# Sparse attention's value products: the two key/value heads in the array's two column halves in turn

## The chip, the cores and the metric

The kernel runs on one core of a Trainium2 chip. A core has a matrix engine (TensorE, PE), a vector engine (VectorE, DVE), a scalar engine (ScalarE, ACT), GpSimd (POOL), and SyncE (SP), which here only issues DMA transfers. Each engine works through its own instruction stream in order and they wait for each other through semaphores. PE loads a stationary operand (a weight load, PEld in the profile) and streams the moving operand past it (a matmul, PE), and writes only to PSUM, which has 8 banks of 128 partitions. The metric is the device time of the whole program in microseconds (us), the median of three runs.

## The reference

Two transformer blocks over 256 positions of width 1024, batch 1. The change lies in the second block's mixer, which adds a sparse attention (NSA) with 8 query heads in 4 groups over 2 key/value heads of width 64, and a gated linear attention (GLA) with 4 heads, each behind a branch projection and a gate:

```python
o_nsa = nsa_attention(q_a, kc, vc, ks_, vs_, kw, vw, gate_a + nsa_gate_b[l], ...)
o_gla = gla(q_b, k_b, v_b, r_b, alpha_b, gla_w_alpha2[l], gla_b_alpha[l], gla_norm_g[l])
g_nsa, g_gla = jnp.split(jax.nn.sigmoid(merge), 2, axis=-1)
mix = g_nsa * (o_nsa @ w_branch_nsa[l]) + g_gla * (o_gla @ w_branch_gla[l])
x = x + (mix @ w_out[l]).astype(x.dtype)
```

Inside `nsa_attention` each query head has three outputs, over compressed keys, selected blocks and a window, added with gates:

```python
o_cmp = jnp.einsum('bhgqn,bnhd->bqhgd', p_cmp.astype(v_cmp.dtype), v_cmp)
...
o_slc = jnp.einsum('bhgqk,bhqkd->bqhgd', p_slc.astype(vg.dtype), vg)
...
o_win = jnp.einsum('bhgqk,bkhd->bqhgd', p_win.astype(vwb.dtype), vwb)
return gb[..., 0:1] * o_cmp + gb[..., 1:2] * o_slc + gb[..., 2:3] * o_win
```

With 256 positions there are 4 blocks of 64 keys, all of them selected, and the window covers 256 positions, so both are dense causal attentions here. GLA works in chunks of 64 positions: `o_intra` (a masked 64x64 product with v) plus `o_inter` (the queries with the state of all chunks before).

## The kernel before

Every large product is split into exact high and low parts (three matmuls, `mm3`); the small attention products run in fp32, each of which the profile records as two passes, a weight load and a matmul each. All work is planned by a `Schedule` that writes steps into one list; each engine's program runs through this list and picks its own steps, so the order on each engine is fixed when the program is built. A step takes PSUM banks through `use`, and PE's `open_bank` waits until the bank's last reader has released it.

Weights come in units of 1 MB through a ring of four slots (`low_f`): SP loads unit u when PE has finished unit u - 4, ACT writes its rounded part (`high`), DVE the rest (`low_r`), each in two halves of 128x1024, and then PE uses it. `planned` loads four row blocks of 128 rows as `(k p) n -> p k n`, so row block k holds rows 128k to 128k + 127.

The stretch of interest is written by `nsa`, woven with `gla` and with a stream of wide projection steps (`fill`: the merge gates, then the GLA branch weights "bg"). A head index n (0 to 7) stands for one query half i = n // 4 (128 queries) and one group g = n % 4, both key/value heads v at once. For each n the steps are:

- `nsa_s` (PE): scores, both value heads in two row halves of the array. DVE adds the slopes and takes maxima, ACT exponentials, DVE (`nsa_w`) the gated weights.
- `nsa_t` (PE): turns these weights into banks 6, 7 and 1 (128x128 blocks, and one 64x128 for the compressed ones). ACT copies them to `WK_f`: the transposed weights, per v at column 2048 + 512v, the compressed ones at 3072.
- `nsa_v` (PE): the value products. For each v: for both branches and each key tile (nk = i + 1 tiles) one product of the values `VSW` (128 rows, 64 columns) with the turned weights, and one of the compressed values `VC2`, which uses 47 rows. Both v write the same 64 partitions `hr` of bank 1 (lower half for even g, upper for odd), v = 0 into columns 0 to 127 and v = 1 into 128 to 255.
- ACT copies 64x256 elements of it to `ONT`, high part, and DVE subtracts for the low part. `head_pair` says where: partitions `hr`, row blocks g // 2 and g // 2 + 2, so that `ONT`'s four row blocks stand in the reference's row order.

After the last head the branch projection "bn" takes `ONT` as stationary operand against the units of `w_branch_nsa_2`.

In GLA, for a pair i of chunks, `gla_t` computes the intra-chunk scores for two row halves p (banks 0 and 1), two products each. `gla_o` computes, for p = 0 and then p = 1: two products with 128 rows (`AT` with `VB`), then for each chunk n = 2i + half two products of 64 rows and 64 columns, queries with `STATE`, into partitions 64half. Chunk 0 has no state, so pair 0 has one such half and pair 1 both.

The names in the rows: `PS` is PSUM; `AR_f` and `AR_r` are one large work area that holds VSW, VC2, ONT, EN, QB, STATE, AT and more; `HT_r` the turned activations; `XN` the GLA output. Shapes such as 128*64 are rows and columns of the stationary operand.

Of the kernel before, what the change touches and what calls it, by code (L numbers as in the profile page):

```python
# [11 lines left out]
ALU = mybir.AluOpType  # L12
# [121 lines left out]
class Schedule:  # L134
# [23 lines left out]

    def plan_wide(self, key, w, c0, n=1024):
        for c in range(c0, c0 + n, 512):  # L160
            for k0 in range(0, w.shape[0] // 128, 4):
                self.planned(key, w, k0, 4, c, 512)
# [14 lines left out]
    def make_plan(self, A):  # L177
# [26 lines left out]
        for key, w in (("bg", A["w_branch_gla_2"][0]), ("bn", A["w_branch_nsa_2"][0])):  # L204
            for c in range(0, 1024, 512):
                self.planned(key, w, 0, 4, c, 512)
# [809 lines left out]
def two_blocks(nc, A, out):  # L1016
    ctx = ExitStack()
    with ctx:
# [105 lines left out]
        VSW = ar(1536, 2, 2, 128)  # L1124
# [135 lines left out]
        def head_pair(n):  # L1260

            i, g = divmod(n, 4)
            hr = slice(64 * (g % 2), 64 * (g % 2) + 64)
            return ONT[hr, g // 2:4:2, i * 128:i * 128 + 128]
# [41 lines left out]
        def tensor_program(eng):  # L1306
# [408 lines left out]
            def gla_t(s):  # L1715
                i = s["i"]
                pe.wait_ge(s_gel, 1)
                for p in range(2):
                    use = U["gt", i, p]
                    rr = slice(64 * p, 64 * p + 64)  # L1720
                    open_bank(use)
                    for q in range(2):
                        m = mm(bank(use)[:, 128 * q:128 * q + 128], EN[rr, q, 128 * i:128 * i + 128],
                               QB[rr, q, 128 * i:128 * i + 128], True, True)
                    m.then_inc(use.full[0], 1)

            def gla_o(s):
# [4 lines left out]
                for p in range(2):  # L1732
                    use = U["go", i, p]
                    open_bank(use)
                    for q in range(2):
                        h = 2 * q + p
                        m = mm(bank(use)[:, 128 * q:128 * q + 128], AT[:, 2 * p + q, :],
                               VB[:, i, 128 * h:128 * h + 128], q == 0, False)
                    for half in range(2):
                        n = 2 * i + half  # L1740
                        if n == 0:
                            continue
                        pe.wait_ge(*U["gs", n - 1].read)
                        for q in range(2):
# [3 lines left out]
                    m.then_inc(use.full[0], 1)  # L1748
# [49 lines left out]
            def nsa_v(s):  # L1798
# [4 lines left out]
                hr = slice(64 * (g % 2), 64 * (g % 2) + 64)  # L1803
# [6 lines left out]
                open_bank(use)  # L1810
                for v in range(2):
                    oo = bank(use)[hr, 128 * v:128 * v + 128]
                    wT = wk(2048 + 512 * v, 512)
                    for br in range(2):
                        for kt in range(nk):
                            j = br * nk + kt
                            mm(oo, VSW[:, br, kt, 64 * v:64 * v + 64], wT[:, 128 * j:128 * j + 128], j == 0, False)
                    m = mm(oo, VC2[0:47, v, :], wk(3072, 128)[0:47, :], False, True)
# [1607 lines left out]
```

## Time and profile before

| | |
|---|---|
| median of 3 runs | 830.67 us (829.7 to 832.2) |
| span of the profiled execution | 829.0 us |
| PE busy | 816.5 us, 98% of the span |
| weight loads busy | 704.3 us, 85% |
| DVE / ACT / POOL busy | 610.5 / 455.6 / 96.6 us |
| DMA | 143.40 MB, mean 173 GB/s |
| granted TensorE clock | 1.000 |
| the stretch with the sparse attention's heads | about 453 to 558 us |

The times come from one profiled execution. PE's matmuls are pipelined: the recorded duration of one is longer than the distance to the next, so costs are read from the distance between starts. The weight loads of short products start in step with their matmuls, so the start of a group of loads tells when its products begin.

### The profile page before, as it was taken

How to read it: one execution, taken by the hardware profiler on the slowest of the kernel's cores; microseconds unless marked ns; L12 is line 12 of the kernel's file. 1: busy time of each engine (PE TensorE's matmuls, PEld its weight loads, DVE VectorE, ACT ScalarE, POOL GpSimd, SP SyncE). 2: the span in 40 equal slices, each digit the busy share in tenths (PEclk: the TensorE clock that was granted, in tenths of full speed). 3: DMA queues.
4: the chain of work that ended last, by engine and by line, in shares of the span. 5: the costliest groups of instructions: out<-in, count | busy, mean ns of one | idle time of the engine just before them, and what ended most of it. 6: DMA issues, size and time to landing. Idle time of an engine off the chain costs nothing.

```text
span 829.0 us, 12090 instructions
## 1 busy us (share of the span) xinstructions
PE 816.5 (98%) x4841; PEld 704.3 (85%) x4841; DVE 610.5 (74%) x966; ACT 455.6 (55%) x804; POOL 96.6 (12%) x106
## 2 busy tenths in 40 slices
PE   7999999999999999999999999999999999999997
PEld 6878888888888888899998777778888999999886
DVE  6878767978877755567578776858568799998744
ACT  6656565735555544454575546554476645544533
POOL 4200000000000000000400000000000455655100
PEclk9999999999999999999999999999999999999999
DMA  9854634555755555374875333244543556555551
GB/s 331 231 174 135 225 119 153 175 189 167 253 173 184 203 189 173 146 249 129 241 218 171 120 102 102 102 151 163 171 150 102 184 172 203 165 192 183 177 199 51
DMA packets 81607, 143.40 MB, mean 173 GB/s; under 512 B 5090, under 2 KB 35840, under 8 KB 81552
## 3 DMA queue, kind: packets, MB, share of 16 engines
q1 hardware_dynamic: 79232, 137.11, 50.7%
q0 software_dynamic: 2160, 5.46, 2.3%
q8 instruction: 38, 0.62, 0.3%
q14 instruction: 17, 0.14, 0.0%
q10 hardware_dynamic: 160, 0.07, 0.0%
HBM read 141.05 MB, written 1.05 MB: 171 GB/s over the span
## 4 chain that ended last, share of the span: by engine, by line
PE 96%; DVE 2%; ACT 1%; DMA 0%; issue 0%; ACTq 0%; DVEq 0%
PE PS L1310 92%; PE PS L1324 4%; ACT WK_f L1928 1%; DMA VR<-in_norm_attn_g_dram 0%; DVE low_r L2439 0%; DVE HT_r L2439 0%; ACT high L1931 0%; DVE WK_f L2443 0%; DVE X L2439 0%; ACT AR_f L1931 0%; DVE WK_f L2447 0%; DVE AR_f L2439 0%; DVE XN L2443 0%; DVE AR_f L2443 0%; DVE WK_f L2439 0%
## 5 line engine op out<-in xcount | busy, mean ns | idle before, releaser
L2439 DVE TENSOR_TENSOR low_r<-low_f,high 128x1024 fp32r<-128x1024 f32 (+1 forms) x256 | 325.7, 1314 | 77.4 <-ACT high L1931 77.2
L1931 ACT ACTIVATE high<-low_f 128x1024 fp32r<-128x1024 f32 (+1 forms) x264 | 257.4, 1024 | 76.0 <-DMA low_f<-in_w_down_dram 35.0
L1310 PE MATMUL PS<-HT_r,high 128*128 128x256 f32 (+2 forms) x1232 | 267.5, 308 | 0.0
L1310 PE MATMUL PS<-high,AR_r 128*128 128x512 f32 (+2 forms) x724 | 214.9, 377 | 0.0
L1310 PEld LDWEIGHTS PS<-HT_r,high 128*128 128x128 f32 (+1 forms) x1232 | 199.7, 190 | 12.2
L1310 PE MATMUL PS<-HT_r,low_r 128*128 128x256 f32 (+1 forms) x712 | 200.9, 282 | 0.0
L1310 PE MATMUL PS<-high,HT_r 128*128 128x512 f32 (+1 forms) x576 | 189.3, 396 | 0.7 <-DVE HT_r L2439 0.4
L1310 PEld LDWEIGHTS PS<-high,AR_r 128*128 128x128 f32 (+1 forms) x724 | 129.2, 181 | 26.4 <-issue 0.5
L1310 PEld LDWEIGHTS PS<-HT_r,low_r 128*128 128x128 f32 (+1 forms) x712 | 135.2, 190 | 0.0
L1310 PE MATMUL PS<-low_r,AR_r 128*128 128x512 f32 (+2 forms) x362 | 134.0, 374 | 0.0
L1310 PEld LDWEIGHTS PS<-high,HT_r 128*128 128x128 f32 x576 | 108.0, 189 | 25.1 <-issue 2.7
L1310 PE MATMUL PS<-low_r,HT_r 128*128 128x512 f32 (+1 forms) x288 | 110.9, 387 | 0.0
L1310 PEld LDWEIGHTS PS<-low_r,AR_r 128*128 128x128 f32 (+1 forms) x362 | 65.5, 181 | 12.1
L3246 POOL TENSOR_TENSOR WK_f<-WK_f 128x512 f32<-128x512 f32 x33 | 53.3, 1616 | 115.2 <-DVE WK_f L2447 113.4
L1310 PEld LDWEIGHTS PS<-low_r,HT_r 128*128 128x128 f32 x288 | 54.7, 190 | 9.3
L1931 ACT ACTIVATE AR_r<-AR_f 128x512 fp32r<-128x512 f32 (+1 forms) x29 | 18.2, 629 | 71.6 <-DVE AR_f L2439 40.6
L2439 DVE TENSOR_TENSOR AR_r<-AR_f,AR_r 128x512 fp32r<-128x512 f32 (+1 forms) x29 | 23.7, 822 | 18.9 <-ACT AR_r L1931 18.9
L1928 ACT ACTIVATE WK_f<-WK_f,st 128x128 f32<-128x128 f32 (+2 forms) x80 | 32.9, 416 | 6.0 <-DVE st L2443 6.0
L1310 PE MATMUL PS<-AR_f 64*128 64x128 f32 (+5 forms) x268 | 31.9, 318 | 0.2 <-ACT AR_f L1931 0.2
L1310 PEld LDWEIGHTS PS<-AR_f 64*128 64x128 f32 (+2 forms) x268 | 24.6, 182 | 8.5 <-issue 6.7
L1931 ACT ACTIVATE AR_f<-PS 128x512 f32<-128x512 f32 (+2 forms) x34 | 18.7, 550 | 21.7 <-PE PS L1310 20.2
L1931 ACT ACTIVATE WK_f<-PS 128x512 f32<-128x512 f32 (+2 forms) x38 | 15.3, 448 | 26.7 <-PE PS L1324 23.9
(173 smaller groups left out, 694.9 us busy)
## 6 DMA issues: line engine op xcount, KB each, us to landing
low_f<-in_w_in_dram SPq DMA_DIRECT2D x39, 1024.0 KB, 5.2
low_f<-in_w_up_dram SPq DMA_DIRECT2D x38, 1024.0 KB, 5.2
low_f<-in_w_down_dram SPq DMA_DIRECT2D x27, 1024.0 KB, 4.9
low_f<-in_w_out_dram SPq DMA_DIRECT2D x8, 1024.0 KB, 5.0
low_f<-in_w_xkv_dram SPq DMA_DIRECT2D x4, 1024.0 KB, 5.7
low_f<-in_w_branch_gla_dram SPq DMA_DIRECT2D x2, 1024.0 KB, 5.0
low_f<-in_w_branch_nsa_dram SPq DMA_DIRECT2D x2, 1024.0 KB, 5.0
low_f<-in_w_xq_dram SPq DMA_DIRECT2D x2, 1024.0 KB, 5.4
```

Source lines behind the costliest of these rows:

```text
L1310: return nc.tensor.matmul(o, l, r, start=start, stop=stop, skip_group_check=True)
L1324: return nc.tensor.transpose(o, i, ident[0:n, 0:n])
L1928: return nc.scalar.activation(o, i, f, bias=bias, scale=scale, accum_out=total)
L1931: return nc.scalar.activation(o, i, ACT.Copy, bias=0.0, scale=1.0)
L2439: return nc.vector.tensor_tensor(o, a, b, op)
L3246: return nc.gpsimd.tensor_tensor(o, a, b, op)
```

## The change

The value products of head n put value head v into column half v of the array: `oo[v]` are the partitions 64v to 64v + 63 of the bank, and both write columns 0 to 127. The products of the two value heads stand in turn. The compressed product uses all 128 rows of `VC2` and of the turned weights, whose other rows are cleared once. The output, now 128x128, is copied and subtracted as one block, and `ONT` has one row block for each g, with the two value heads as its halves. `by_value_head` loads the branch weights in that row order, each unit as two loads of 64 partitions. In `gla_t` and `gla_o` the products of the row halves stand in turn, and `gla_o`'s 128-row products come ahead of all its 64-row ones.

```diff
@@ class Schedule
+    def by_value_head(self, key, w, c):
+
+        def half(v):
+            src = w[256 * v:256 * v + 256, c:c + 512].rearrange("(g d) n -> d g n", d=64)
+            return lambda a: v3(a, 4, 512)[64 * v:64 * v + 64], src
+
+        self.unit(key, 4, 512, [half(v) for v in range(2)])
@@ make_plan
-        for key, w in (("bg", A["w_branch_gla_2"][0]), ("bn", A["w_branch_nsa_2"][0])):
-            for c in range(0, 1024, 512):
-                self.planned(key, w, 0, 4, c, 512)
+        for c in range(0, 1024, 512):
+            self.planned("bg", A["w_branch_gla_2"][0], 0, 4, c, 512)
+        for c in range(0, 1024, 512):
+            self.by_value_head("bn", A["w_branch_nsa_2"][0], c)
@@ head_pair
-            hr = slice(64 * (g % 2), 64 * (g % 2) + 64)
-            return ONT[hr, g // 2:4:2, i * 128:i * 128 + 128]
+            return ONT[:, g, i * 128:i * 128 + 128]
@@ gla_t, PE
                 for p in range(2):
-                    use = U["gt", i, p]
-                    rr = slice(64 * p, 64 * p + 64)
-                    open_bank(use)
-                    for q in range(2):
+                    open_bank(U["gt", i, p])
+                for q in range(2):
+                    for p in range(2):
+                        use = U["gt", i, p]
+                        rr = slice(64 * p, 64 * p + 64)
                         m = mm(bank(use)[:, 128 * q:128 * q + 128], EN[rr, q, 128 * i:128 * i + 128],
                                QB[rr, q, 128 * i:128 * i + 128], True, True)
-                    m.then_inc(use.full[0], 1)
+                        if q == 1:
+                            m.then_inc(use.full[0], 1)
@@ gla_o, PE
-                        m = mm(bank(use)[:, 128 * q:128 * q + 128], AT[:, 2 * p + q, :],
-                               VB[:, i, 128 * h:128 * h + 128], q == 0, False)
-                    for half in range(2):
-                        n = 2 * i + half
-                        if n == 0:
-                            continue
-                        pe.wait_ge(*U["gs", n - 1].read)
-                        for q in range(2):
+                        mm(bank(use)[:, 128 * q:128 * q + 128], AT[:, 2 * p + q, :],
+                           VB[:, i, 128 * h:128 * h + 128], q == 0, False)
+                for half in range(2):
+                    n = 2 * i + half
+                    if n == 0:
+                        continue
+                    pe.wait_ge(*U["gs", n - 1].read)
+                    for q in range(2):
+                        for p in range(2):
+                            use = U["go", i, p]
                             m = mm(bank(use)[64 * half:64 * half + 64, 128 * q:128 * q + 128],
                                    QB[64 * p:64 * p + 64, q, 64 * n:64 * n + 64], STATE[n][64 * p:64 * p + 64, q, :],
                                    False, True)
-                    m.then_inc(use.full[0], 1)
+                            if half == q == 1:
+                                m.then_inc(use.full[0], 1)
@@ nsa_v, PE
+                oo = [bank(use)[64 * v:64 * v + 64, 0:128] for v in range(2)]
+                for br in range(2):
+                    for kt in range(nk):
+                        j = br * nk + kt
+                        for v in range(2):
+                            wT = wk(2048 + 512 * v, 512)
+                            mm(oo[v], VSW[:, br, kt, 64 * v:64 * v + 64], wT[:, 128 * j:128 * j + 128], j == 0, False)
                 for v in range(2):
-                    oo = bank(use)[hr, 128 * v:128 * v + 128]
-                    wT = wk(2048 + 512 * v, 512)
-                    for br in range(2):
-                        for kt in range(nk):
-                            j = br * nk + kt
-                            mm(oo, VSW[:, br, kt, 64 * v:64 * v + 64], wT[:, 128 * j:128 * j + 128], j == 0, False)
-                    m = mm(oo, VC2[0:47, v, :], wk(3072, 128)[0:47, :], False, True)
+                    m = mm(oo[v], VC2[:, v, :], wk(3072, 128), False, True)
@@ nsa_v, ACT and DVE
-                cp(head_pair(n).hi, halves(bank(use)[hr, 0:256])).then_inc(s_onh, 1)
+                cp(head_pair(n).hi, bank(use)[:, 0:128]).then_inc(s_onh, 1)
...
-                tt(o.lo, halves(bank(use)[hr, 0:256]), o.hi, ALU.subtract).then_inc(use.read[0], 1)
+                tt(o.lo, bank(use)[:, 0:128], o.hi, ALU.subtract).then_inc(use.read[0], 1)
@@ cmp_g, DVE
-                    nc.vector.memset(VC2[0:47], 0.0).then_inc(*own.up())
+                    nc.vector.memset(VC2, 0.0).then_inc(*own.up())
                     nc.vector.memset(wk(3840, 128), 0.0).then_inc(*own.up())
+                    nc.vector.memset(wk(3072, 128)[64:128], 0.0).then_inc(*own.up())
```

How PE's stream changes at `gla_o` of pair 0, with the waits that stand there (`read0` and `read1` are the banks' releases; the first and second rows of 128x128 are `AT` products, the 64x128 ones those with `STATE`, and `nsa_s` of head 3 follows). Before:

```order
1977 L1310 MATMUL PS<-AR_f 128x128 [waits read0,gla_masked]
1978 L1310 MATMUL PS<-AR_f 128x128
1979 L1310 MATMUL PS<-AR_f 64x128 x2
1980 L1310 MATMUL PS<-AR_f 128x128 [waits read1]
1981 L1310 MATMUL PS<-AR_f 128x128
1982 L1310 MATMUL PS<-AR_f 64x128 x2
1983 L1310 MATMUL PS<-AR_f 128x128 [waits read4]
```

After:

```order
1975 L1318 MATMUL PS<-AR_f 128x128 [waits read0,gla_masked]
1976 L1318 MATMUL PS<-AR_f 128x128
1977 L1318 MATMUL PS<-AR_f 128x128 [waits read1]
1978 L1318 MATMUL PS<-AR_f 128x128
1979 L1318 MATMUL PS<-AR_f 64x128 x4
1980 L1318 MATMUL PS<-AR_f 128x128 [waits read4]
```

The products of one shape now stand together. At `nsa_v` the rows read alike before and after (6 products in the first query half, 10 in the second, each with a 64x128 output, behind the same waits for banks 1, 7 and 6); there only the operands and the place of the output change.

SP's stream at the branch weights, before:

```order
26 L3361 DMA low_f<-in_w_branch_gla_dram 128x4x512 x2
27 L3361 DMA low_f<-in_w_branch_nsa_dram 128x4x512 x2
28 L3361 DMA low_f<-in_w_out_dram 128x4x512 x4
29 L3361 DMA low_f<-in_w_xq_dram 128x4x512 x2
30 L3361 DMA low_f<-in_w_xo_dram 128x4x512 x2
```

and after:

```order
26 L3373 DMA low_f<-in_w_branch_gla_dram 128x4x512 x2
27 L3373 DMA low_f<-in_w_branch_nsa_dram 64x4x512 x4
28 L3373 DMA low_f<-in_w_out_dram 128x4x512 x4
29 L3373 DMA low_f<-in_w_xq_dram 128x4x512 x2
30 L3373 DMA low_f<-in_w_xo_dram 128x4x512 x2
```

Two loads have become four, of half the partitions each, at the same place.

## Rows read from the trace of the kernel before

**Rows 1.** The page: busy us (share) xinstructions; the chain by engine.
```profile
PE 816.5 (98%) x4841; PEld 704.3 (85%) x4841; DVE 610.5 (74%) x966; ACT 455.6 (55%) x804; POOL 96.6 (12%) x106
...
PE 96%; DVE 2%; ACT 1%; DMA 0%; issue 0%; ACTq 0%; DVEq 0%
```

**Rows 2.** Stretches: length, busy PE, PEld, DVE, ACT, POOL, then clock, DMA.
```profile
458.00:560.00 102.00, 101.87 (x586) 79.18 (x586) 72.38 (x177) 57.95 (x144) 0.00 (x0) 1.00 0.35 114
560.00:612.00 52.00, 52.00 (x288) 45.00 (x287) 35.53 (x50) 24.29 (x36) 0.57 (x1) 1.00 0.52 172
```

**Rows 3.** Timeline, weight loads, head 2's value products: start, us, line, operation, tiles, count.
```profile
486.68 0.41 PEld L1310 LDWEIGHTS PS<-WK_f,AR_f 128*64 128x64 f32 x4 [0.33 <-issue]
487.26 0.19 PEld L1310 LDWEIGHTS PS<-WK_f,AR_f 47*64 47x64 f32 x2 [0.17 <-issue]
487.62 0.41 PEld L1310 LDWEIGHTS PS<-WK_f,AR_f 128*64 128x64 f32 x4 [0.17 <-issue]
...
488.56 0.19 PEld L1310 LDWEIGHTS PS<-high,HT_r 128*128 128x128 f32 x1 [0.17 <-issue]
```

**Rows 4.** Timeline, weight loads, head 5's value products.
```profile
528.79 0.85 PEld L1310 LDWEIGHTS PS<-WK_f,AR_f 128*64 128x64 f32 x8 [0.17 <-issue]
529.81 0.19 PEld L1310 LDWEIGHTS PS<-WK_f,AR_f 47*64 47x64 f32 x2 [0.17 <-issue]
...
531.54 0.19 PEld L1310 LDWEIGHTS PS<-high,HT_r 128*128 128x128 f32 x1 [0.17 <-issue]
```

**Rows 5.** Timeline, PE and weight loads, gla_o of pair 0 (four separate windows).
```profile
476.26 2.71 PE L1310 MATMUL PS<-AR_f 128*128 128x128 f32 x18
...
476.79 0.41 PEld L1310 LDWEIGHTS PS<-AR_f 64*64 64x64 f32 x4
477.37 0.19 PEld L1310 LDWEIGHTS PS<-AR_f 128*128 128x128 f32 x1 [0.17 <-issue]
...
478.59 0.19 PEld L1310 LDWEIGHTS PS<-AR_f 64*128 64x128 f32 x2 [0.17 <-issue]
```

**Rows 6.** The same, gla_o of pair 1.
```profile
504.16 2.85 PE L1310 MATMUL PS<-AR_f 128*128 128x128 f32 x26
...
504.70 0.42 PEld L1310 LDWEIGHTS PS<-AR_f 64*64 64x64 f32 x8
505.29 0.19 PEld L1310 LDWEIGHTS PS<-AR_f 128*128 128x128 f32 x1 [0.17 <-issue]
...
506.52 0.19 PEld L1310 LDWEIGHTS PS<-AR_f 64*128 64x128 f32 x2 [0.17 <-issue]
```

**Rows 7.** Timeline, PE, the starts of gla_t of pair 0 and pair 1.
```profile
462.79 0.39 PE L1310 MATMUL PS<-AR_f 64*128 64x128 f32 x2
...
491.50 0.39 PE L1310 MATMUL PS<-AR_f 64*128 64x128 f32 x2
```

**Rows 8.** The page's DMA issues; timeline, SP and ACT, first sparse-branch weight unit.
```profile
low_f<-in_w_branch_nsa_dram SPq DMA_DIRECT2D x2, 1024.0 KB, 5.0
...
539.19 0.37 SPq L3361 DMA_DIRECT2D low_f<-in_w_branch_nsa_dram  x1
...
549.16 2.00 ACT L1931 ACTIVATE high<-low_f 128x1024 fp32r<-128x1024 f32 x2
```

**Rows 9.** Timeline, DVE and PE, up to head 5's turned weights.
```profile
516.03 2.36 DVE L2439 TENSOR_TENSOR low_r<-low_f,high 128x1024 fp32r<-128x1024 f32 x2 [3.50 <-ACT high L1931]
...
521.93 0.41 DVE L2439 TENSOR_TENSOR AR_r<-PS,AR_r 64x256 fp32r<-64x256 f32 x1
...
523.80 0.38 DVE L2447 SCALAR_TENSOR_TENSOR WK_f<-WK_f,st,cst 128x15 f32<-128x15 f32 x2
...
524.48 0.63 PE L1324 MATMUL PS<-cst,WK_f 128*128 128x128 f32 x4
```

**Rows 10.** Timeline, DVE, around the two gla_t: subtractions that free bank 1.
```profile
461.68 0.42 DVE L2439 TENSOR_TENSOR AR_r<-PS,AR_r 64x256 fp32r<-64x256 f32 x1
463.53 0.42 DVE L2439 TENSOR_TENSOR AR_f<-PS,cst 128x256 f32<-128x256 f32 x1 [1.44 <-PE PS L1310]
...
490.29 0.42 DVE L2439 TENSOR_TENSOR AR_r<-PS,AR_r 64x256 fp32r<-64x256 f32 x1
```

More of the change, by code:

```diff
@@ L1802, in nsa_v @@
                 use = U["no", n]
-                hr = slice(64 * (g % 2), 64 * (g % 2) + 64)
                 for v in range(2):
@@ L2317, in nsa_v @@
                 use = U["no", n]
-                hr = slice(64 * (g % 2), 64 * (g % 2) + 64)
                 act.wait_ge(*use.full)
@@ L3111, in nsa_v @@
                 use = U["no", n]
-                hr = slice(64 * (n % 2), 64 * (n % 2) + 64)
                 o = head_pair(n)
                 dve.wait_ge(s_onh, n + 1)
-                tt(o.lo, halves(bank(use)[hr, 0:256]), o.hi, ALU.subtract).then_inc(use.read[0], 1)
+                tt(o.lo, bank(use)[:, 0:128], o.hi, ALU.subtract).then_inc(use.read[0], 1)
             def mix_turn(s):
```

## The prediction

> **What bounds the kernel now.** I read the page's busy shares and its chain first. TensorE (PE) is busy 98% of the 829.0 us span and makes up 96% of the chain that ended last [rows 1]. In the two stretches that hold the changed work and what follows it, 458 to 560 us and 560 to 612 us, PE is busy 101.87 of 102 us and 52.00 of 52 us, at a granted clock of 1.00, which is the 2.4 GHz level, with VectorE (DVE) at 71% and 68% and ScalarE (ACT) lower [rows 2]. The list of PE's waits shows none between 458 and 560 us. So a microsecond less of PE work there is a microsecond off the span, as long as nobody makes PE wait in its place; the rest of this text is about how much PE work goes, and who then is late.
>
> **Value products (nsa_v).** The eight heads' products come in two sizes. Read the weight loads, which stand one per pass; every fp32 product is two passes. In a head of the first query half, four passes with 128 rows take 0.58 us until the first 47-row load (486.68 to 487.26), two passes of the 47-row compressed product take 0.36 (to 487.62), then the same again for the other value head; the next stage starts at 488.56, so the block takes 1.88 us [rows 3]. In a head of the second half eight passes take 1.02 us (528.79 to 529.81) and the block 2.75 us, to 531.54 [rows 4]. The difference, 0.44 us for four passes, gives 0.11 us for each pass that follows another of the same shape. A pass behind a change of shape costs more: 0.36 for two instead of 0.22, so 0.14 for the change. All of this runs in one column half: both value heads write the partitions hr. There are four blocks of each size.
>
> After the change each value head has its own column half and the compressed product has 128 rows like the others. Do two column halves work at the same time? The trace of before shows it in the sums of the linear attention (gla_o). For chunk pair 0 a block of four 64-row, 64-column passes lasts from 476.79 to 477.37, 0.58 us; there only one column half is written [rows 5]. For chunk pair 1 the same row half writes both column halves, eight passes, and these last from 504.70 to 505.29, 0.59 us [rows 6]. Eight in the time of four, with different streamed operands and one PSUM bank, and although the four of one column half stand in the program ahead of the four of the other. I take this as the price for nsa_v, whose tiles differ only in having 128 rows.
>
> Then a block lasts as long as one value head's passes: 6 in the first half, 0.58 + 2 x 0.11 = 0.80 us, and 10 in the second, 1.02 + 2 x 0.11 = 1.24 us. Saved: 4 x (1.88 - 0.80) + 4 x (2.75 - 1.24) = 4.3 + 6.0 = **10.3 us**. The low bound is that halves don't overlap and only the shape changes go: 12 passes 0.58 + 8 x 0.11 = 1.46, 20 passes 1.02 + 12 x 0.11 = 2.34, so 0.42 and 0.41 us a block, 3.3 us in all. I take the upper value, because rows 6 are the nearer case.
>
> The Trainium skill speaks against this. Its page "TensorE: Matmul & The Clock Gate", Part 3, "The mechanism", says that a weight load overlaps running matmuls only where its row group differs; by that the sum would be 3.3 us, the low bound. Rows 6 disagree: one row group, two column groups, twice the passes in the same time.
>
> **Sums and scores of the linear attention (gla_o, gla_t).** gla_o now does both row halves' 128-row products first, then all 64-row ones. For pair 0 it takes 478.59 - 476.26 = 2.33 us [rows 5]. After: eight wide passes, of which four take 0.53 (476.26 to 476.79), so 0.53 + 0.44 = 0.97, then both row halves together 0.58: 1.55, saved 0.78. For pair 1, 506.52 - 504.16 = 2.36 us [rows 6]; after, 0.97 + 0.59 = 1.56 if all four quarters of the array work together, saved 0.80, and 0.44 less if only two do. Together **1.6 us**, low end 1.1. gla_t is only reordered. In before its two row halves already start together: two matmuls begin at 491.50 [rows 7]. So it gives nothing.
>
> The same section of the same page says that matmuls start and end strictly in program order. By it, gla_t's two row halves, which stand one behind the other, would run in series now, and the new order would save 4 x 0.11 us in each of two blocks, 0.9 us more. Rows 7 show the second half starting at once, so I leave it out of the sum.
>
> **What costs nothing.** One memset more and one larger on DVE, once, before the first head: between nothing and the 0.4 us of DVE's 64x256 subtraction [rows 10], a larger operation; I take nothing, since DVE's share leaves it room, and keep the 0.4 for the range. Each branch weight unit of the sparse attention is now two loads of 64 partitions, 512 KB each. The first is issued at 539.19, lands about 5.0 us later, at 544.2, and ACT begins to split it at 549.16 [rows 8]. That leaves 5.0 us, less 1.5 by which PE will be earlier in between; it covers a landing that takes 1.7 times as long. Beyond that ACT would wait, and PE only once the split units ahead of it are used up. The copies of a head's output are 128x128 instead of 64x256, so a little shorter on ACT and DVE.
>
> **Who is late next.** PE's lead only counts where its next wait is already met. Three places fail.
> - Head 5's turned weights. PE starts them at 524.48 and DVE hands them over at 524.18 (523.80 + 0.38), at the end of a stretch in which DVE works without a gap from 516.03 [rows 9]. That stretch starts when ACT has made its halves after head 5's exponentials, so it hangs on head 4's turns, not on head 4's value products. The 1.5 us saved there turns into a wait, except for the shorter subtraction (0.42 for 64x256; I estimate 0.1 less): lost 1.4 us.
> - Both blocks of gla_t need PSUM bank 1, freed by DVE's subtraction. The first ends at 461.68 + 0.42 = 462.10; PE started at 462.79 and would like 461.71 now: lost 0.3 us. The second ends at 490.71, PE would like 491.50 - 1.08 = 490.42: lost 0.2 us [rows 7, 10].
> Elsewhere DVE itself waits for PE at these places (1.44 us at 463.53 [rows 10]) and moves with it. After the last head the stretch is PE's alone [rows 2], and loads, splits and evacuations follow PE's releases, so the lead stays.
>
> **The sum.** 10.3 + 1.6 - 1.9 = **10.0 us**: 829.0 becomes 819.0 us in the profiled execution. The runs' median is 830.67, 1.7 above that span, so I predict 820.7 us.
>
> **Rivals.**
> - The gain turns into more waits. If DVE sets the pace in heads 6 and 7 as in head 5, two more savings of 1.5 us go: 7.0 us, 823.7. For it: the pace of DVE's chain in head 5 [rows 9]. Against it: no wait of PE in the list, and DVE's mean of 71% [rows 2]. 11%.
> - The column halves don't overlap for tiles with 128 rows: 3.3 + 1.1 less about 0.4 at head 5, so 4.0 us, 826.7. Rows 6 speak against it, but with 64 rows. 6%. The change wouldn't then do what it says.
> - Slower: going from one column half to the other costs as a change of shape does, 0.14 us. The order has 64 products in turn, each 0.22 + 0.14 = 0.36 us: 6 make 2.16 and 10 make 3.6 against 1.88 and 2.75, so 4.5 us more, less 1.6 of gla_o: 833.6. It decides from about 0.08 us for each change ((3.3 + 1.6) / 64). Against it: in rows 6 such a change costs nothing. 3%.
> - Matmuls in strict order before, and gla_t gains 0.9: 819.8. 2%. It is the page's rule above, priced from the rows.
>
> **How the numbers follow.** The forecast, with savings from 8.5 (only two quarters at once in gla_o, 0.4 less, and 1.1 us more of waits or of memsets) to 11.9 us (no wait at all), has 77%; the remaining 1% is anything else. The range takes in the forecast's own spread and the first rival: 818.5 to 824.5 us. A measurement of this kernel tells about 0.3%, 2.5 us, from no change. Faster by more than that are the forecast, the first two rivals and the last: 0.95, of which I give 0.02 to runs that fall short; so 0.93 faster, 0.04 the same, 0.03 slower.
>
> **What would show it.** In the profile after, nsa_v's loads come in pairs and a block lasts 0.8 and 1.25 us; if 1.46 and 2.34, the halves don't overlap; if over 2 and 3, a change of half is paid. gla_o's blocks last 1.55 us each. In PE's list of waits a wait of about 1.4 us for DVE's product at head 5's turns is new; two or three such say the first rival. ACT waiting for the loads of the branch weights would say that 64 partitions load slowly. The prediction is wrong if these waits grow beyond what the blocks give.

## The result, and the profile after

The changed kernel takes **821.43 us** (median of 4 runs, 820.03 to 821.45) against 831.04 us (median of 4, 829.7 to 832.2) for the kernel before, measured beside it. The ratio is 0.9886, with a 95% interval of 0.9874 to 0.9898. The forecast was 820.7 us. The profiled execution spans 819.6 us, where the forecast had 819.0.

The page of the changed kernel has the engines' busy time and the chain by engine, to be held against [rows 1]:

```profile
PE 804.7 (98%) x4841; PEld 697.8 (85%) x4841; DVE 609.3 (74%) x967; ACT 453.5 (55%) x804; POOL 96.5 (12%) x106
...
PE 92%; DVE 4%; ACT 3%; issue 0%; DMA 0%; ACTq 0%; DVEq 0%
```

PE has as many instructions as before and 11.8 us less busy time. The chain has handed 4% of the span to DVE and ACT: somewhere PE waits for them now. (At a wait the chain goes on along the releaser's own work, so these 4% are far more than the wait itself.) The stretches of [rows 2] and PE's list of waits (us in total, times, longest) say where:

```profile
458.00:560.00 102.00, 99.90 (x632) 80.08 (x630) 77.50 (x185) 59.02 (x146) 0.00 (x0) 1.00 0.41 124
```

```profile
PE PS L1332 <- DVE WK_f L2459: 2.1, 2, 1.5
...
PE PS L1318 <- DVE AR_r L2451: 0.6, 2, 0.3
```

Before, PE was busy for 101.87 us of that stretch; now 2.1 us are idle. One wait of 1.5 us is for DVE's turned weights (the other of that line, 0.5 us, is head 0's and was there before), and two of 0.3 and 0.2 us are for bank 1, which DVE frees.

**The value products.** Weight loads of head 2 and of head 5, the two sizes of [rows 3] and [rows 4]:

```profile
484.84 0.63 PEld L1318 LDWEIGHTS PS<-WK_f,AR_f 128*64 128x64 f32 x12 [0.33 <-issue]
485.64 0.19 PEld L1318 LDWEIGHTS PS<-high,HT_r 128*128 128x128 f32 x1 [0.17 <-issue]
...
524.19 1.07 PEld L1318 LDWEIGHTS PS<-WK_f,AR_f 128*64 128x64 f32 x20 [0.17 <-issue]
525.43 0.19 PEld L1318 LDWEIGHTS PS<-high,HT_r 128*128 128x128 f32 x1 [0.17 <-issue]
```

Twelve passes end after 485.64 - 484.84 = 0.80 us, twenty after 525.43 - 524.19 = 1.24. The eight blocks are 4 x 0.80 and 4 x 1.24 us, against 1.88 and 2.75 before: 10.3 us less.

**gla_o.** PE's start of pair 0 and of pair 1, and the first loads of the stage behind each, as in [rows 5] and [rows 6] (windows of PE and of the weight loads; the last row is a window of 0.06 us, the moment at which pair 1's 64x64 passes begin):

```profile
475.19 0.60 PE L1318 MATMUL PS<-AR_f 128*128 128x128 f32 x4
...
476.75 0.63 PEld L1318 LDWEIGHTS PS<-AR_f 64*128 64x128 f32 x9 [0.17 <-issue]
```

```profile
500.44 0.72 PE L1318 MATMUL PS<-AR_f 128*128 128x128 f32 x5
...
502.04 0.52 PEld L1318 LDWEIGHTS PS<-AR_f 64*128 64x128 f32 x6 [0.17 <-issue]
```

```profile
501.42 0.16 PEld L1318 LDWEIGHTS PS<-AR_f 64*64 64x64 f32 x4
```

Pair 0 takes 1.56 us (2.33 before) and pair 1 takes 1.60 (2.36 before): 1.5 us less. In the window of 0.06 us four 64x64 loads begin. The row doesn't name the quarters of the array; that all four work at once follows from the time: pair 1's 16 such passes take 0.62 us (501.42 to 502.04), and four in one quarter took 0.58 [rows 5].

**Who is late.** DVE and PE up to head 5's turned weights, answering to [rows 9]:

```profile
511.55 2.36 DVE L2451 TENSOR_TENSOR low_r<-low_f,high 128x1024 fp32r<-128x1024 f32 x2 [3.43 <-ACT high L1944]
514.02 2.19 DVE L2459 SCALAR_TENSOR_TENSOR XN<-XN,st,glag 128x128 f32<-128x128 f32 x8
516.25 1.29 DVE L2451 TENSOR_TENSOR XN<-XN,AR_f 128x512 f32<-128x512 f32 x2
517.46 0.28 DVE L2451 TENSOR_TENSOR AR_r<-PS,AR_r 128x128 fp32r<-128x128 f32 x1
...
519.20 0.37 DVE L2459 SCALAR_TENSOR_TENSOR WK_f<-WK_f,st,cst 128x15 f32<-128x15 f32 x2
...
519.88 1.17 PE L1332 MATMUL PS<-cst,WK_f 128*128 128x128 f32 x9 [1.53 <-DVE WK_f L2459]
```

DVE works without a gap from 511.55 to 519.57 us, and PE starts 0.3 us after it. The subtraction of a head's output, 128x128 now, takes 0.28 us; it was 0.41.

**Bank 1**, as in [rows 7] and [rows 10]: DVE's subtraction, then PE's start of gla_t, for pair 0.

```profile
462.41 0.29 DVE L2451 TENSOR_TENSOR AR_r<-PS,AR_r 128x128 fp32r<-128x128 f32 x1
...
462.85 0.90 PE L1318 MATMUL PS<-AR_f 64*128 64x128 f32 x11 [0.34 <-DVE AR_r L2451]
```

**The loads**, as in [rows 8]: the page's row, and the issue of the first unit's two halves.

```profile
low_f<-in_w_branch_nsa_dram SPq DMA_DIRECT2D x4, 512.0 KB, 6.0
...
533.08 1.35 SPq L3373 DMA_DIRECT2D low_f<-in_w_branch_nsa_dram  x2
```

A half of 64 partitions lands 6.0 us after its issue, where one piece of 128 took 5.0. No wait of PE or ACT in the lists is for it.

**One step before the first head.** PE's last compressed product and the next stage's first, in the kernel before and in the changed one:

```profile
432.48 0.22 PE L1310 MATMUL PS<-high,AR_r 128*30 128x128 f32 x1
432.54 0.45 PE L1310 MATMUL PS<-HT_r,high 128*128 128x256 f32 x2
```

```profile
433.05 0.22 PE L1318 MATMUL PS<-high,AR_r 128*30 128x128 f32 x1
433.24 0.47 PE L1318 MATMUL PS<-HT_r,high 128*128 128x256 f32 x2
```

The gap is 0.06 us before and 0.19 after. The stage needs a weight half that DVE finishes here, and DVE's memsets stand ahead of that half.

**A stretch to compare by.** These rows also show that the changed kernel's trace lies some 0.6 us later than before's by then. That comes from the first 27 us, in which nothing was changed (an experiment below bears this out). So I compare the kernels by the stretch from PE's start of head 0's turned weights to its first product of the next attention (xat_s, two operands of the AR tile, 256 columns), which holds all changed work but the memset:

```profile
453.49 0.73 PE L1324 MATMUL PS<-cst,WK_f 128*128 128x128 f32 x5 [0.54 <-DVE WK_f L2447]
...
609.84 0.60 PE L1310 MATMUL PS<-AR_f 128*128 128x256 f32 x2
```

```profile
454.23 0.74 PE L1332 MATMUL PS<-cst,WK_f 128*128 128x128 f32 x5 [0.54 <-DVE WK_f L2459]
...
600.66 0.60 PE L1318 MATMUL PS<-AR_f 128*128 128x256 f32 x2
```

609.84 - 453.49 = 156.35 us before and 600.66 - 454.23 = 146.43 in the changed kernel: **9.9 us less**, where the sum of the forecast is 10.0.

### The profile page after: what moved, and what is told of

It is laid out like the page before. It is cut to its first block, busy times and chain, and to the rows that moved or that the text cites. A ratio compares the mean times of both kernels' runs of the same rounds, so it can differ in the third digit from the quotient of the medians.

```text
span 819.6 us, 12095 instructions
## 1 busy us (share of the span) xinstructions
PE 804.7 (98%) x4841; PEld 697.8 (85%) x4841; DVE 609.3 (74%) x967; ACT 453.5 (55%) x804; POOL 96.5 (12%) x106
## 4 chain that ended last, share of the span: by engine, by line
PE 92%; DVE 4%; ACT 3%; issue 0%; DMA 0%; ACTq 0%; DVEq 0%
PE PS L1318 89%; PE PS L1332 3%; ACT WK_f L1941 1%; DVE low_r L2451 1%; ACT high L1944 1%; DMA VR<-in_norm_attn_g_dram 0%; ACT WK_f L1944 0%; DVE WK_f L2455 0%; DVE WK_f L2459 0%; DVE XN L2451 0%; DVE XN L2459 0%; DVE HT_r L2451 0%; DVE AR_f L2459 0%; ACT L1938 0%; DVE X L2451 0%
## 5 line engine op out<-in xcount | busy, mean ns | idle before, releaser
L1944 ACT ACTIVATE high<-low_f 128x1024 fp32r<-128x1024 f32 (+1 forms) x264 | 257.3, 1024 | 78.6 <-DMA low_f<-in_w_down_dram 34.8
```

Of the source, the lines that this page charges most:

```text
L1944: return nc.scalar.activation(o, i, ACT.Copy, bias=0.0, scale=1.0)
```

## The experiments

The theory has four parts: what a block of value products costs by its passes and its changes of shape; that column halves (and quarters) of the array work at the same time; that DVE's chain takes 1.4 us back at head 5; and that loads and gla_t's order give nothing. The table has all kernels that ran. "Stretch" is the one just named, and "blocks" are the two sizes of value products. The kernel before took 830.44 and 830.75 us (medians) beside the timed runs of the experiments and 829.94 (one run) beside in_threes, gla_t_old and old_loads. The expectations count from head 0's turned weights to the span's end instead, which adds the 218.9 to 219.3 us behind the stretch; that part has the same instructions in all kernels.

| kernel | median us | span | start of head 0 | stretch | against changed | blocks |
|---|---|---|---|---|---|---|
| before | 831.04 | 829.0 | 453.49 | 156.35 | +9.9 | 1.88, 2.75 |
| changed | 821.43 | 819.6 | 454.23 | 146.43 | | 0.80, 1.24 |
| after_again | 821.10 | 818.7 | 453.37 | 146.48 | 0.0 | 0.80, 1.24 |
| shape_only | 828.02 | 826.2 | 453.90 | 153.42 | +7.0 | 1.46, 2.32 |
| v_after_v | 823.77 | 821.9 | 453.83 | 149.21 | +2.8 | 1.08, 1.95 |
| in_twos | 821.15 (one run) | 819.4 | 453.81 | 146.65 | +0.2 | 0.81, 1.29 |
| in_threes | 822.74 (one run) | 820.9 | 454.31 | 147.77 | +1.3 | 1.07, 1.51 |
| rows47 | 820.77 (one run) | 819.0 | 452.86 | 147.17 | +0.7 | 0.95, 1.39 |
| no_gla | 822.03 | 820.6 | 453.55 | 147.78 | +1.3 | 0.80, 1.24 |
| gla_t_old | 820.27 (one run) | 818.4 | 452.97 | 146.29 | -0.15 | 0.80, 1.24 |
| old_loads | 821.30 (one run) | 819.5 | 454.12 | 146.48 | 0.0 | 0.80, 1.24 |
| gla_r_later | 819.56 | 817.2 | 453.12 | 144.91 | -1.5 | 0.80, 1.24 |
| both_later | 819.13 | 817.3 | 453.49 | 144.90 | -1.5 | 0.80, 1.24 |

### One shape for all tiles, one column half (shape_only)

```diff
-                m = mm(oo, VC2[0:47, v, :], wk(3072, 128)[0:47, :], False, True)
+                m = mm(oo, VC2[:, v, :], wk(3072, 128), False, True)
-                nc.vector.memset(VC2[0:47], 0.0)
+                nc.vector.memset(VC2, 0.0)
+                nc.vector.memset(wk(3072, 128)[64:128], 0.0)
```

> The kernel before with one thing changed: the compressed product has 128 rows (its operands' rows beyond 47 are zero), so all weight tiles of a head's value products have one shape. Both value heads still write one column half, one after the other, and the sums of the linear attention are as before. Theory (0.14 us for each change of tile shape): blocks of 1.46 and 2.34 us instead of 1.88 and 2.75, 3.3 us less work; 0.4 us of it is lost to a longer wait at head 5's turned weights and 0.15 to the added memset, so the span is 826.2 us against 829.0 and the median 828.0. Rival (the 47-row product is slow for another reason, such as where it stands at a block's end): the blocks stay at 1.88 and 2.75 and the span at 829.1. If the whole gain of the change came from the shapes and none from the two column halves, this kernel would be at 821.

Measured: 828.02 us, ratio 0.9968 [0.9955, 0.9981], span 826.2. The weight loads of head 2:

```profile
486.27 1.28 PEld L1310 LDWEIGHTS PS<-WK_f,AR_f 128*64 128x64 f32 x12 [0.33 <-issue]
487.73 0.19 PEld L1310 LDWEIGHTS PS<-high,HT_r 128*128 128x128 f32 x1 [0.17 <-issue]
```

Twelve passes take 1.46 us where the kernel before took 1.88 for the same twelve. Each change between 128-row and 47-row tiles thus costs 0.14 us, as worked out from [rows 3]; there were three in a block. PE's wait at head 5's turned weights grew by 0.4 us, also as expected. The Trainium skill, "TensorEngine Tiling (Array Packing)", "Key Properties", says that a change of tiling mode drains TensorE; the trace agrees that a change costs time, though it can't tell a drain from another cost of the change, and the number is this one.

The shapes alone bring 156.35 - 153.42 = 2.9 us of the 9.9, just what was expected; the other 7 us come with the second column half and gla_o.

### The value heads one after the other, in two column halves (v_after_v)

```diff
-                for br in range(2):
-                    for kt in range(nk):
-                        for v in range(2):
-                            mm(oo[v], VSW[:, br, kt, 64 * v:64 * v + 64], ...)
-                for v in range(2):
-                    m = mm(oo[v], VC2[:, v, :], wk(3072, 128), False, True)
+                for v in range(2):
+                    for br in range(2):
+                        for kt in range(nk):
+                            mm(oo[v], VSW[:, br, kt, 64 * v:64 * v + 64], ...)
+                    m = mm(oo[v], VC2[:, v, :], wk(3072, 128), False, True)
```

> The changed kernel with another program order inside a head's value products: all products of value head 0 (column half 0), then all of value head 1 (column half 1), instead of in turn. Theory (the two column halves take their work independently of how it is interleaved in the program, as the sums of the linear attention did in the kernel before with four passes behind four): blocks stay at 0.80 and 1.24 us, span 819.6, median 821.4. Rival (passes start in program order, and only neighbours of different column halves overlap): blocks of 1.46 and 2.34 us, 7.0 us more work, of which about 1.1 falls into the wait at head 5's turned weights: span 825.5, median 827.3. Values between would say that the second half can run ahead only by some passes; 6 passes stand ahead in heads 0 to 3 and 10 in heads 4 to 7.

Measured: 823.77 us, ratio 0.9919 [0.9902, 0.9935]; 2.3 us above the changed kernel (2.8 in the stretch). Neither answer was right; it is the case between them that the expectation names last. Blocks last 1.08 and 1.95 us, between "the same" and "in series". Stretches of head 0 and of head 4, PE's value products only (length, busy time, how many):

```profile
458.32:458.60 0.28, 0.28 (x3) 1.00 0.00 0
458.60:459.40 0.80, 0.80 (x12) 1.00 0.00 0
510.17:510.88 0.71, 0.71 (x6) 1.00 1.03 378
510.89:512.12 1.23, 1.23 (x16) 1.00 0.05 18
```

(The counts take in passes still running at a stretch's start.) In head 0 three passes start alone, 0.16 and 0.11 us apart, and from 458.60 on passes start twice as often: value head 1 has joined, while three of value head 0's six passes hadn't started. In head 4 seven start alone (the seventh at 510.88, on the edge of the stretch), again with three of ten left. A pass whose column half is free can thus start ahead of three waiting ones and not of more. The price is the lone time, 0.28 and 0.71 us a block. Over eight heads that is 4.0 us, of which 2.8 reach the end of the stretch: the waits for bank 1 (0.6 us) are gone, and the one at head 5 is 0.8 us instead of 1.5.

The changed gla_o qualifies the "three". In pair 1 the first pass of column half 1 stands in the program behind eight passes of column half 0, four for each row half, and yet, as the four loads and the block's time show, all four quarters begin within 0.06 us, with six of the eight still waiting. So three can't be the limit over all waiting passes. It fits both kernels if it counts those that wait for the same rows: three in each row half there, and here, where a pass takes all 128 rows, three in all. No run tests this reading by itself.

### Groups of two and of three (in_twos, in_threes)

The diff is that of in_twos; in_threes has 3 for the 2 and counts the compressed product as the last of a value head's row.

```diff
-                for br in range(2):
-                    for kt in range(nk):
-                        j = br * nk + kt
-                        for v in range(2):
+                for j0 in range(0, 2 * nk, 2):
+                    for v in range(2):
+                        for j in range(j0, j0 + 2):
+                            br, kt = divmod(j, nk)
                             mm(oo[v], VSW[:, br, kt, 64 * v:64 * v + 64], ...)
```

> The changed kernel with the value products in groups: two products (four passes) of value head 0, two of value head 1, and so on, instead of one and one. In v_after_v value head 1's first pass started after 3 of 6 passes of value head 0 in heads 0 to 3, and after 7 of 10 in heads 4 to 7, thus as soon as no more than three passes that stood ahead of it were still waiting. Theory (a pass for a free column half can start over at most three waiting ones): with four ahead, one running and three waiting, nothing is lost; the first passes of both halves start within 0.1 us, blocks 0.80 and 1.24 us. Rival (each pass that stands ahead costs something): blocks of 0.85 to 1.0 and 1.35 to 1.6 us.

> The changed kernel with the value products in groups of three (six passes): three of value head 0, three of value head 1, then the rest. Theory (a pass for a free column half can start over at most three waiting ones): value head 1 starts after three passes of value head 0, 0.27 us late, and stays so: blocks of 1.08 us in heads 0 to 3 (there the order is that of v_after_v) and 1.24 + 0.27 = 1.51 us in heads 4 to 7. Rival (in v_after_v it was something else, such as value head 0's last passes being near): the start is late by another amount, or each further group costs it again, 1.8 us or more.

Measured: in_twos has 0.81 and 1.29 us, in_threes 1.07 and 1.51. Two views of in_threes at head 4: the loads, and the stretches before and after value head 1 joins (length, busy PE, PEld, DVE, ACT, clock, DMA).

```profile
510.58 1.34 PEld L1318 LDWEIGHTS PS<-WK_f,AR_f 128*64 128x64 f32 x20 [0.35 <-issue]
512.09 0.19 PEld L1318 LDWEIGHTS PS<-high,HT_r 128*128 128x128 f32 x1 [0.17 <-issue]
```

```profile
510.58:510.85 0.27, 0.27 (x3) 0.27 (x3) 0.00 (x0) 0.00 (x0) 1.00 1.04 387
510.85:512.09 1.24, 1.24 (x20) 1.07 (x18) 0.00 (x0) 0.00 (x0) 1.00 0.41 144
```

With six ahead, three start alone and the loss is 0.27 us, to the hundredth what "three waiting" gives, and it isn't paid again at the second group. (In the short blocks the order is that of v_after_v, and so is their time within 0.01 us.) With four ahead (in_twos) the short blocks lose 0.01 us; the long ones lose 0.05 us, which the rule doesn't explain and I leave open.

The Trainium skill, in "TensorE: Matmul & The Clock Gate", Part 3, "The mechanism", gives TensorE a reorder window of 64, through which weight loads are pulled ahead, and says in the same section that matmuls start strictly in program order. If the window held for whole passes of a free column half, v_after_v would have lost nothing; by strict order it would have lost 0.66 and 1.1 us a block. The runs show 0.28 and 0.71: passes do start out of order, here ahead of three waiting ones.

### The compressed product with 47 rows again (rows47)

```diff
-                    m = mm(oo[v], VC2[:, v, :], wk(3072, 128), False, True)
+                    m = mm(oo[v], VC2[0:47, v, :], wk(3072, 128)[0:47, :], False, True)
-                nc.vector.memset(VC2, 0.0)
+                nc.vector.memset(VC2[0:47], 0.0)
-                nc.vector.memset(wk(3072, 128)[64:128], 0.0)
```

> The changed kernel with the compressed product of 47 rows again (and without the added memset), in its two column halves. Theory (each change of tile shape drains the array, 0.14 us): blocks of 0.94 and 1.38 instead of 0.80 and 1.24 us, 1.1 us more over eight heads, of which head 4's 0.14 is covered by the wait at head 5's turned weights; the step of 0.14 us at 433 us goes. Counted from head 0's turned weights: 365.4 + 1.0 = 366.4 us. Rival (the change costs each column half in turn, or the next stage pays once more): blocks of 1.1 and 1.5 us, or more.

Measured: blocks of 0.95 and 1.39 us, 0.7 us more in the stretch; 1.0 was expected. The loads of head 4:

```profile
508.90 0.85 PEld L1318 LDWEIGHTS PS<-WK_f,AR_f 128*64 128x64 f32 x16 [0.35 <-issue]
509.92 0.19 PEld L1318 LDWEIGHTS PS<-WK_f,AR_f 47*64 47x64 f32 x4 [0.17 <-issue]
510.29 0.19 PEld L1318 LDWEIGHTS PS<-high,HT_r 128*128 128x128 f32 x1 [0.17 <-issue]
```

One change of shape, 0.15 us, paid once for both halves and once a block. Eight make 1.2 us of work, of which 0.7 reach the end: the waits for bank 1 (0.6 us in the changed kernel, 0.2 here) and at head 5 (1.5 and 1.4) take the rest. I had forgotten the former.

### Without the linear attention's part (no_gla, gla_t_old)

no_gla has gla_o and gla_t of the kernel before, gla_t_old gla_t alone; the orders are those of the diff above the prediction, taken back.

```diff
-                for q in range(2):
-                    for p in range(2):
+                for p in range(2):
+                    open_bank(U["gt", i, p])
+                    for q in range(2):
```

> The changed kernel with the linear attention's gla_t and gla_o in the order of the kernel before; the value products stay changed. Theory: gla_o takes 2.33 and 2.36 us again instead of 1.57 and 1.6, gla_t gives nothing; PE is 0.8 us later from the first gla_o on, so the 0.3 us wait for bank 1 at the second gla_t goes. Span 819.6 + 1.55 - 0.3 = 820.9, median 822.7. Rival (passes start strictly in program order, so gla_t's new order also gives 0.9): 821.8. Rival (gla_o's gain is swallowed by later waits): 819.6.

> The changed kernel with gla_t alone in the order of the kernel before (row half 0 with its four passes, then row half 1); gla_o stays changed. With v_after_v's finding four passes ahead, one running and three waiting, are just what a pass can overtake. Theory: both row halves start within 0.05 us as in the kernel before, 365.3 us counted from head 0's turned weights. Rival (matmuls start in program order): each gla_t 0.44 us longer, 366.2 us.

Measured: no_gla 822.03 us, ratio 0.9899 [0.9884, 0.9914], the stretch 1.3 us longer than in the changed kernel: 1.5 for gla_o, less the 0.15 that the old order of gla_t gives back (gla_t_old, next). The expectation had 1.25, but it let the wait for bank 1 at the second gla_t go. In the trace row half 1 still starts 0.20 us behind row half 0 there. Counted to the span's end it is 1.7, because two passes at 761 us, in untouched work, took 0.4 us longer in that profile; more on that below.

gla_t_old: the stretch is 0.15 us shorter than in the changed kernel. So the new order of gla_t gives nothing, as [rows 7] said, and even costs a little. PE's first gla_t in gla_t_old:

```profile
460.86 0.39 PE L1318 MATMUL PS<-high,HT_r 128*128 128x512 f32 x1
461.18 0.70 PE L1318 MATMUL PS<-AR_f 64*128 64x128 f32 x4
```

PE goes on 0.32 us after the start of the matmul ahead, without a wait, and no wait for bank 1 is left in its list. With the old order row half 0 may start in bank 0 while bank 1 is still being read, and row half 1 joins later: 0.32 us here, after which passes start twice as often. That head start brings only 0.15 us to the end, so most of the 0.6 us of waits stays lost. In the new order the first product of each row half stands in front, and both banks must be free. So the waits for bank 1 are only in a small part of the reordering's own making.

### The branch weights in one piece (old_loads)

```diff
-            self.by_value_head("bn", A["w_branch_nsa_2"][0], c)
+            self.planned("bn", A["w_branch_nsa_2"][0], 0, 4, c, 512)
```

> The changed kernel with the sparse attention's branch weights loaded in one piece of 128 partitions each, as in the kernel before. Their rows then don't answer to the order of the heads' outputs, so the output is another; the work is the same. It tells what the two loads of 64 partitions cost. Theory: nothing, since ACT splits the unit microseconds after it has landed; counted from head 0's turned weights the span stays at 365.3 us. Rival (the slower landing, 6.0 against 5.0 us, delays a split that PE waits for): up to 1 us less.

Measured: the stretch is that of the changed kernel, 146.48 us. The loads in two pieces cost nothing, though they land 0.9 us later (5.1 against 6.0 us).

### DVE's gla_r behind head 5's weights (gla_r_later)

```diff
             def nsa_s(s):
                 ...
                 ts(st[:, o:o + 6], st[:, o:o + 6], -1.0, None, ALU.mult).then_inc(s_nmx, 1)
+                if n == 6:
+                    gla_r()
```

(gla_r is no step of DVE's table any more; its ten operations are the same.)

> The changed kernel, except that DVE runs its gla_r step (ten operations, 3.4 us) after its nsa_s of head 6 instead of ahead of its nsa_w of head 5. Theory (DVE's stretch of gla_r sets the new wait at head 5's turned weights): DVE hands head 5's weights over at about 516.1 instead of 519.6 us, PE's wait of 1.5 us there goes, span 818.1, median 819.9. Rival A (the wait hangs on ACT's exponentials of head 5, not on gla_r): the wait and the span stay, 819.6. Rival B (DVE's or ACT's chain sets the pace in heads 6 and 7 as well): the wait at head 5 goes, but 0.7 to 1.5 us of waits appear at head 6's or 7's turned weights or at gla_T, span 818.8 to 819.6.

Measured: 819.56 us, ratio 0.9866 [0.9851, 0.9881], the stretch 1.5 us shorter. DVE and PE at head 5:

```profile
514.90 0.37 DVE L2459 SCALAR_TENSOR_TENSOR WK_f<-WK_f,st,cst 128x15 f32<-128x15 f32 x2
...
517.99 2.19 DVE L2459 SCALAR_TENSOR_TENSOR XN<-XN,st,glag 128x128 f32<-128x128 f32 x8
...
517.15 1.03 PE L1332 MATMUL PS<-cst,WK_f 128*128 128x128 f32 x8
```

DVE is ready at 515.27, PE starts at 517.15 without a wait, and gla_r runs behind. Nothing came back at heads 6 and 7 or at gla_T. So DVE's gla_r set the wait, and the first rival of the prediction (waits in heads 6 and 7) had no ground even with PE 1.5 us earlier.

### The memset too, and the changed kernel again (both_later, after_again)

```diff
             def cmp_g(s):
-                    nc.vector.memset(wk(3072, 128)[64:128], 0.0).then_inc(*own.up())
             def cmp_o(s):
                 ...
                 else:
+                    nc.vector.memset(wk(3072, 128)[64:128], 0.0)
                     cp(VC2[0:15, 0, :], bank(use)[0:15, 0:64])
```

> The changed kernel with two DVE steps moved: gla_r runs after nsa_s of head 6 (as in gla_r_later), and the memset that the change added (rows 64 to 127 of the compressed weights) stands in DVE's cmp_o of c = 1 instead of in cmp_g, where it delays the weight half that PE waits for at 433 us. Theory: counted from head 0's turned weights, 1.3 us less than the changed kernel, as in gla_r_later; ahead of them 0.14 us less (the step at 433 us goes). Median 821.4 - 1.45 = 820.0, or 819.4 counted from the median of gla_r_later. Rival (the 0.14 us at 433 us is no effect of the memset, or it comes back where the memset now stands): the step stays or another of its size appears, median as gla_r_later, 819.6.

> The changed kernel once more, unaltered, on the chip and beside the runs of both_later. Expected median 821.4 us, span 819.6 less what its start-up (the first 27 us) differs. If the start-up of an unaltered kernel varies by more than 0.5 us, differences of profiled spans below that are to be counted from head 0's turned weights on, not from the span's start.

Measured on one chip: both_later **819.13 us**, ratio 0.9861 [0.9847, 0.9876]; after_again 821.10 us, ratio 0.9887 [0.9871, 0.9904]. both_later has the lowest median of this study, though gla_r_later's runs (818.48 to 820.24 us) overlap with its own (818.88 to 819.28). Its 1.5 us in the stretch are gla_r's. The step at 433 us is gone:

```profile
432.46 0.22 PE L1318 MATMUL PS<-high,AR_r 128*30 128x128 f32 x1
432.52 0.45 PE L1318 MATMUL PS<-HT_r,high 128*128 128x256 f32 x2
```

The gap is 0.06 us again, as in the kernel before, and no other appears where the memset stands now. The traces of the other kernels say the same: the gap is 0.19 to 0.20 us in all ten that have the memset at its first place, and 0.06 in rows47, which has none. What is left in PE's list for the stretch is head 0's wait and the two for bank 1:

```profile
PE PS L1318 <- DVE AR_r L2451: 0.6, 2, 0.4
...
PE PS L1332 <- DVE WK_f L2459: 0.5, 1, 0.5
```

after_again is the same program as the changed kernel and reaches head 0 at 453.37 instead of 454.23 us: 0.9 us of difference without any cause in the code. In the stretch the two agree within 0.05 us.

## Why the prediction was right, and where it was off

- **What bounds the kernel: right.** PE's saved work went straight into the span, apart from the waits.
- **Value products: right.** 10.3 us forecast, 10.3 measured: 0.80 and 1.24 us a block, as worked out by passes. The upper value, not the bound of 3.3 us.
- **The ground for it was narrower than I thought.** From [rows 6] I took that column halves overlap even when "the four of one column half stand in the program ahead of the four of the other", and made no use of the order. Four ahead means one running and three waiting, which is just what v_after_v shows to be the limit. With six or ten ahead, the overlap is partly lost. So the interleaved order of the change, which my sum doesn't mention as a cause, is worth 2.8 us in the stretch and 2.3 by the medians.
- **gla_o: right,** 1.5 us against 1.6; the four quarters work at once.
- **gla_t: right that the new order gives nothing,** but I didn't see that it makes row half 0 wait for bank 1 as well, which costs 0.15 us. The waits themselves were in the sum.
- **Head 5: right.** 1.4 us forecast; from the start of the product ahead to the start of the turned weights it is now 1.92 us (517.96 to 519.88) and was 0.52. Its cause is shown by gla_r_later.
- **Bank 1: right,** 0.34 + 0.22 = 0.56 us against 0.5.
- **"One memset more ... I take nothing, since DVE's share leaves it room": this step failed.** It cost 0.13 us. DVE's mean share says nothing of one place. There DVE has no gap ahead of the weight half that PE waits for. The term lay within the bound of 0.4 that I kept for the range.
- **Loads, copies: right,** nothing.
- **The sum.** 10.3 + 1.5 - 1.4 - 0.6 = 9.8 us, and the stretch is 9.9 us shorter; the forecast was 10.0.
- **From 819.0 to 819.6 us.** The profiled span gained 9.4 us and not 10.0: 0.1 us went to the memset and 0.6 to the start-up, which has no cause in the code (after_again reached head 0 0.9 us sooner); 0.2 us came back behind the stretch. The median of 821.43 is 0.7 us above the forecast: 0.6 are the span's, and it lies 1.8 us above the span where I had 1.7.
- **The rivals.** Waits in heads 6 and 7: none came. Halves that don't overlap, and a charge for a change of half: the blocks exclude both. Strict program order: gla_t_old excludes it; the old order would have cost 0.9 us and gave 0.15. One slip in the chances: the forecast, the first two rivals and the last add up to 0.96, not 0.95.

## What to carry to other kernels

Small products gain from column halves as from row halves, if tiles of one shape follow one another and the products for the two halves alternate; each change of shape costs about 0.14 us, and a half whose work stands more than four passes behind in the program starts late (seen with tiles of 128 rows). When PE's work shrinks, look in the trace at each hand-over of the next engine for the slack that it has there; an engine's mean share hides both a 1.5 us wait and a 0.13 us one. A step that nobody needs yet, like gla_r here, is best put behind the hand-over.

## What the runs showed of the hardware that I had not expected

- TensorE starts a pass whose part of the array is free ahead of passes that wait for another part, but not over any number of them. With tiles of 128 rows it was three at most: value head 1 joined after 3 of 6 and after 7 of 10 passes (v_after_v), after 3 of 6 again (in_threes), and at once with four ahead (in_twos). With tiles of 64 rows it was six, three in each row half (gla_o of pair 1).
- The first 27 us of an unaltered program differ by up to 0.9 us between profiles (head 0 at 453.37 and 454.23 us), and the kernels here range from 452.86 to 454.31 us. In the 146 us behind that point the same program repeats within 0.05 us. Small effects are better read between two such points than from the span.
- In four of the thirteen profiles two or so of PE's passes take longer than their neighbours of the same kind, each time at another moment and with no wait on record. The kernel before has it at 769 us, where two passes take 0.65 us until the next one starts instead of 0.46; no_gla has it at 761 us with 0.82, gla_t_old at 759 us and gla_r_later at 798 us. The cause is open. It moves a span by 0.2 to 0.4 us:

```profile
769.28 0.81 PE L1310 MATMUL PS<-high,AR_r 128*128 128x512 f32 x2
769.93 0.40 PE L1310 MATMUL PS<-low_r,AR_r 128*128 128x512 f32 x1
```

```profile
760.76 0.98 PE L1318 MATMUL PS<-high,AR_r 128*128 128x512 f32 x2
761.58 0.40 PE L1318 MATMUL PS<-low_r,AR_r 128*128 128x512 f32 x1
```

- 512 KB to 64 partitions took 6.0 us from issue to landing when two such loads were issued one after the other, 1024 KB to 128 partitions 5.0.
